# Gate and up products of sixteen experts: the eight high products of a block, then its eight low ones

## What is computed

```
gate, idx = lax.top_k(aff.T, cap)              # 16 experts, cap = 128 sample + 64 prompt tokens
xe  = h[idx]
hid = silu(einsum('ecd,edf->ecf', xe, w_gate)) * einsum('ecd,edf->ecf', xe, w_up)
ye  = einsum('ecf,efd->ecd', hid, w_down) * gate[..., None]
out = zeros_like(h).at[idx.reshape(-1)].add(ye.reshape(-1, D))
```

## Time and profile before

| | |
|---|---|
| median of three runs | 2502.47 us |
| the profiled execution | 2503.91 us |
| its span on the core | 2502.1 us |
| mean granted clock of PE | 0.986 |
| PE busy | 2428.1 us (97%) |
| PEld busy | 2170.2 us (87%) |
| DVE, ACT, POOL busy | 1678.2, 1459.8, 160.1 us |

### The profile page before, as it was taken

How to read it: one execution, slowest core, us unless ns; L and a number is a source line. 1 busy time by engine, 2 the same in 40 slices (tenths; PEclk the granted TensorE clock), 3 DMA queues, 4 the chain that set the end, 5 groups by cost and what they waited for, 6 DMA issues and landing times.

```text
span 2502.1 us, 42899 instructions
## 1 busy us (share of the span) xinstructions
PE 2428.1 (97%) x16262; PEld 2170.2 (87%) x16262; DVE 1678.2 (67%) x2520; ACT 1459.8 (58%) x2054; POOL 160.1 (6%) x168
## 2 busy tenths in 40 slices
PE   7999999989959999999999999999999999999997
PEld 6888867767659999898999989899998989999896
DVE  6355289854777667676666767676666767666676
ACT  4332188877645656655555656556565655656574
POOL 0000000000010101011010101101010110101010
PEclk9999999989979999999999999999999999999998
DMA  7353254354366767677676767767676776767695
GB/s 248 123 179 111 62 163 163 110 203 162 118 247 235 253 224 259 229 251 253 231 253 225 254 228 255 249 238 245 225 259 229 257 238 241 251 226 260 223 330 208
DMA packets 104548, 545.26 MB, mean 218 GB/s; under 512 B 11344, under 2 KB 19920, under 8 KB 54800
## 3 DMA queue, kind: packets, MB, share of 16 engines
q1 hardware_dynamic: 97072, 518.19, 58.9%
q0 software_dynamic: 7392, 25.96, 4.5%
HBM read 503.21 MB, written 40.89 MB: 217 GB/s over the span
## 4 chain that ended last, share of the span: by engine, by line
PE 69%; DVE 2%; ACT 1%; DMA 1%; issue 0%; POOL 0%; SPq 0%; DVEq 0%; ACTq 0%; POOLq 0%
PE ex_gate_ps L1938 16%; PE ex_up_ps L1938 16%; PE ex_gate_ps L1940 7%; PE ex_up_ps L1940 7%; PE ex_down_ps L1952 2%; PE ex_down_ps L1955 2%; PE ex_down_ps L1953 2%; PE ex_down_ps L1954 2%; PE ex_down_ps L1956 2%; PE ex_up_ps L1952 2%; PE ex_up_ps L1954 2%; PE ex_up_ps L1955 2%; PE ex_up_ps L1956 2%; PE ex_up_ps L1953 2%; PE ex_turn_ps L1914 0%; DMA fi_x<-acc_scratch 0%
## 5 line engine op out<-in xcount | busy, mean ns | idle before, releaser
L1793 DVE TENSOR_TENSOR ex_w_lo<-ex_w,ex_w_hi 128x2048 fp32r<-128x2048 f32 x384 | 879.9, 2292 | 450.3 <-ACT ex_w_hi L1705 444.2
L1705 ACT ACTIVATE ex_w_hi<-ex_w 128x2048 fp32r<-128x2048 f32 x384 | 733.5, 1910 | 209.4 <-PE ex_down_ps L1956 106.8
L1938 PE MATMUL ex_gate_ps<-ex_xt,ex_w_hi 128*128 128x384 f32 x2048 | 593.9, 360 | 1.8 <-DVE ex_xt L1799 1.8
L1938 PE MATMUL ex_up_ps<-ex_xt,ex_w_hi 128*128 128x384 f32 x2048 | 592.1, 359 | 0.0
L1940 PE MATMUL ex_gate_ps<-ex_xt,ex_w_lo 128*128 128x192 f32 x2048 | 513.6, 251 | 0.0
L1940 PE MATMUL ex_up_ps<-ex_xt,ex_w_lo 128*128 128x192 f32 x2048 | 512.7, 250 | 0.0
L1940 PEld LDWEIGHTS ex_gate_ps<-ex_xt,ex_w_lo 128*128 128x128 f32 x2048 | 392.3, 192 | 0.6
L1940 PEld LDWEIGHTS ex_up_ps<-ex_xt,ex_w_lo 128*128 128x128 f32 x2048 | 391.2, 191 | 0.0
L1938 PEld LDWEIGHTS ex_gate_ps<-ex_xt,ex_w_hi 128*128 128x128 f32 x2048 | 385.6, 188 | 2.5 <-issue 1.9
L1938 PEld LDWEIGHTS ex_up_ps<-ex_xt,ex_w_hi 128*128 128x128 f32 x2048 | 384.4, 188 | 0.0
L1725 ACT ACTIVATE ex_gate_low<-ex_gate_ps 128x384 f32<-128x384 f32 x128 | 63.0, 492 | 208.1 <-PE ex_gate_ps L1940 208.1
(11 more groups left out here) (298 smaller groups left out, 4011.4 us busy)
## 6 DMA issues: line engine op xcount, KB each, us to landing
ex_w<-in_w_experts SPq DMA_DIRECT2D x384, 1024.0 KB, 4.8
pj_w<-in_w_in SPq DMA_DIRECT2D x54, 512.0 KB, 3.7
pj_xr<-in_xt SPq DMA_DIRECT2D x12, 512.0 KB, 6.4
o_scratch<-ld_out SPq DMA_DIRECT2D x24, 256.0 KB, 4.1
at_bias<-in_near_bias SPq DMA_DIRECT2D x4, 1536.0 KB, 8.8
q_p<-in_x SPq DMA_DIRECT2D x12, 512.0 KB, 4.4
acc_scratch<-k_p SPq DMA_DIRECT2D x12, 512.0 KB, 5.3
h_scratch<-q_p SPq DMA_DIRECT2D x12, 512.0 KB, 2.9
```

The costliest lines, as they stand in the source:

```text
L1705: act.activation(w_hi[:, c % SLOTS, :], w[:, c % SLOTS, :], ACT.Copy).then_inc(hi_w, 1)
L1793: dve.tensor_tensor(w_lo[:, c % SLOTS, :], w[:, c % SLOTS, :], w_hi[:, c % SLOTS, :].bitcast(F32), ALU.subtract).then_inc(lo_w, 1)
L1938: nc.tensor.matmul(out[:, b, 0:2 * CAP], w_hi[:, slot, f], xt[:, k, :, :].rearrange("p h c -> p (h c)"), start=k == 0, stop=False)
```

## The change

Within a block the order of the sixteen matmuls changes. Before, the loop over the eight pieces issued a high and a low product for each piece. Now one loop issues the eight high products and a second one the eight low ones. The operands, the shapes and the number of instructions stay. The first product of a block still clears the bank, the last one is still a low product, and it raises the same semaphore.

```
                     for b in range(BLOCKS):
-                        for k in range(DT):
-                            f = slice((k * BLOCKS + b) * P, (k * BLOCKS + b + 1) * P)
+                        blocks = [slice((k * BLOCKS + b) * P, (k * BLOCKS + b + 1) * P) for k in range(DT)]
+                        for k, f in enumerate(blocks):
                             nc.tensor.matmul(out[:, b, 0:2 * CAP], w_hi[:, slot, f],
                                              xt[:, k, :, :].rearrange("p h c -> p (h c)"), start=k == 0, stop=False)
+                        for k, f in enumerate(blocks):
                             last = nc.tensor.matmul(out[:, b, 0:CAP], w_lo[:, slot, f], xt[:, k, 0, :],
                                                     start=False, stop=k == DT - 1)
                     last.then_inc(chunk_done, 1)
```

## The result

The changed kernel is slower: median 2510.92 us of seven runs (2509.84 to 2513.13), against 2503.04 us of seven runs before (2501.69 to 2505.68). The ratio is 1.0033, 95% interval 1.0022 to 1.0044, so 5.5 to 11 us, about a third of a per cent. The forecast was 2491 us, with 2484 to 2504 as its range.

The account below looks back on a forecast made before the run. PE alone was taken to bound the kernel. 3,584 low products saving 3.3 ns each gave 11.8 us, less 0.3 given back: 2503.9 - 11.5 = 2492.4, or 2491 us on the median's scale, range 2484 to 2504.

Parts of the forecast that it names:

- The cover of the sums and of the weights: Gate and up chunks: chunk sums and weight transfers stay early enough, so PE gets no idle time ahead of the lines.
- the split of the pair: Gate and up products: a pair's 284.4 ns divided into 170.6 for the high product and 113.8 for the low one.
- about 5 ns of latency that is paid once in a run: Low runs: part of each exposed load's 113.8 ns, beyond 109 ns of pace, would be paid by the first load alone.
- fifteen places: High products right behind a 512-column stream, their weights loaded in time; mean 170.6 ns to the next low product.
- The second source: An expert's last low product to line 1953: 340 ns less a 227 ns stream, giving 113 for the low product.
- (a): Transposes of 128 columns, showing loads in a row behind short streams: 110 ns a piece, near but not the same form.
- (b): The router's pair of 16-column matmuls: the second, a load behind a load, priced at 110 to 115 ns.
- the forecast's own case: Low runs: a later low product costs 108.5 to 112.4 ns, total 2484 to 2497.5 us, chance 0.61.
- x: Price of each of the seven low products behind another low one in a block, taken as 110.5 ns.
- Rival 2: Low runs slower: each slot waits for its load and one more hand-over, 118.5 ns, 17 us added, 2519; chance 0.10.
- Rival 1: Low runs: no change, the load behind a low product costs 113.8 ns wherever it stands, 2502.5 us; chance 0.26.
- Rival 3: Low runs much faster: loads overlap, price towards the 85 ns stream, 103 us off, 2399 us; chance 0.03.

Follow-up runs that it names:

- Low128_run: The changed kernel's runs of eight, but low products stream 128 columns instead of 192, leaving out part of the work; 2511.79 us in one run.
- gate_only: Against the kernel before, only gate chunks in runs of eight, up chunks still high and low in turn; 2508.82 us, ratio 1.0022.

## Why the prediction was wrong

**What bounds the kernel** was right: PE alone, no other engine, no transfer, before and after. The cover of the sums and of the weights held: no idle time ahead of the lines.

**The failed step is the split of the pair**, "384 columns take 170.6 ns" and so "a low product holds the engine for 113.8 ns", together with the "about 5 ns of latency that is paid once in a run" that came out of it. The 170.6 came from fifteen places, and all fifteen stand right behind a run of 512 columns. They are not the settled price: behind the same 512 columns the changed kernel's high run goes 171, 175, 178, 185, 176, 182, 173. Settled it is 173.3. The second source, 340 - 227 = 113, had the same flaw: it took the settled 227 for the first stream behind an exposed load, where experiments show first streams of a run to be a few ns longer.

In the prediction's terms a changed block is 8 x 170.6 + 113.8 + 7 x 110.5 = 2,252 ns. It takes 2,293. Of the 41 ns between them the high products make 36 to 39, depending on the reckoning (1,401 to 1,404 ns instead of 1,365), and the low ones 2 to 5 (889 to 892 instead of 887).

The prediction's own rows held another split: loads 109 ns apart behind a low product, which leaves 284.4 - 109 = 175.4 for the high one. The 4.8 ns between 113.8 and 109 were read as a latency of the load. There was none to save seven times a block: a low product in a long run costs 111.7, which is 0.6 ns more than in turn if the high product there is put at 173.3, and 3.4 ns more by the load starts (108.3).

**What came on top** was priced at nothing: "high products stay at 170.6". With high products at 173.3 in turn, the first three of a high run, 202 - 25, 176 and 182, cost some 15 ns more than three settled ones; the fit over the run lengths gives 13. By that fit a block loses 13 + 8 x 0.57 = 17.6 ns, times 512 blocks 9.0 us. Measured are 7.9 us between the medians. By the load starts the same 18 ns are a loss on the low products and a small gain on the high ones.

**Bounds and sources.** The transposes (a), 110 ns a piece, were a form of their own, and the router's pair (b) allowed 110 to 115 for the second of two. From each a price was taken off for a 512-column stream (231 ns, and 227 to 232), but the changed kernel's first such streams behind the exposed loads of a low run start 224 to 236 ns apart from the second on. With that range (a) is 109 to 112 a piece and (b)'s second product 106 to 118, so (b) decided nothing between 110.5 and 113.8. The low gaps of the changed kernel average 111.6. That is inside the forecast's own case (108.5 to 112.4), which stood for 2484 to 2497.5 us, and yet the kernel is slower: x alone didn't decide the time. What lay outside the bounds was the price of the other product.

**The rivals.** Rival 2 had the sign, slower, and the chance 0.10. The half of its mechanism that is a wait for the same columns of the bank falls by the alternating banks. The other half, a hand-over paid at each load behind a load, isn't excluded: it was priced at 4.7 ns, and the load starts show 3.3. Rival 1, an exposed load costs the same wherever it stands, is near for the low product if that costs 111.1 in turn (111.7 in a run), and not if it costs 108.3. Rival 3 needed 85 ns and got 111.7.

The Trainium skill, "TensorE: Matmul & The Clock Gate", section "Back-to-back issue gap", gives 81 ns as the sustained spacing of pairs of load and matmul at 128 columns. Low128_run contradicts it with a mean of 111.6. By the same section of the Trainium skill the gap of an isolated matmul of N columns at the full clock is N / 2.4 + 2.5, an estimate of 162.5 ns at 384 columns. The high runs, which are not isolated matmuls, settle at 173.3.

**The test I set myself** separated the cases: high products 171 apart if right, 175 and more if the first step was wrong. They were at 173 when settled and at 176 and 182 ahead of that. The loads of line 1941 start 111 to 112 ns apart behind the first one's 108, between "right" (110 to 111) and rival 1 (113 to 114). The time from first gate to first down product was to fall to about 72.1 us and rose to 73.37.

**Left open** is what in PE makes the steps, the slow start and the dearer low products behind low ones. The runs show that the order of the pieces and the banks have no part in it, and that the slow start shrinks when the load hardly sticks out. That the gaps of the changed kernel repeat this closely, whatever DVE, ACT and the transfers do beside them, speaks against these. That instructions might arrive late in low runs wasn't tried.

## What to carry to other kernels

Where each matmul has its own load of weights, reordering long and short products didn't hide more loads in these runs: every short one still exposed one. Here the order in turn was the cheapest of all that were tried with 192 columns. Take the price of a matmul from a long run of equal gaps, never from the first one behind another kind, and check it against the distance of the load starts: here the two differed by 5 ns, and the forecast took the difference for a saving. A step of 2 ns in a pair of matmuls decides 0.3% of this kernel, so a forecast built on such a difference needs that difference at the same column counts and in the same pattern.

## What the runs showed that was not expected

- Shortening a product can cost time. With 128 low columns instead of 192 the pair takes 286.7 ns instead of 284.4, as it does with 208: a step and not a slope.
- Nearly all chunk times are whole multiples of 13.33 ns (32 columns at 2.4 GHz): 4,573 is 343, 4,587 is 344, 4,613 is 346, 4,680 is 351, 4,693 is 352, 5,707 is 428 of them. The exceptions are 4,551, the order in turn with 160 or 192 columns, with 341.3, and the chunks of gate_only. In turn the gaps repeat over several pairs, and these stretches are whole multiples again: three pairs with 192 columns (285, 282 and 287 ns in rounded starts, 853.3 together, 64 of them), two with 128, 208 or 224 (573.3, 43), four with 256 (1,173.3, 88). So a mean pair comes in steps. Why the time comes in such units, no run explains.
- With 24 low products a run, whose program has 52,115 instructions instead of 42,899, PE waited at the start of 14 experts for some 2.5 us, which the profile puts down to issue, and the matmuls behind ran at the lower granted clock for some 4 us. That is why that kernel took 2858.2 us, where its chunks alone would make about 2,800. The wait, one such start in the timeline, and a window behind it:

```profile
PE ex_gate_ps L1942 <- issue: 34.1, 14, 2.6
```
```profile
848.31 0.39 PE L1961 MATMUL ex_up_ps<-ex_w_lo,ex_ht 128*128 128x512 f32 x1
851.22 0.64 PE L1942 MATMUL ex_gate_ps<-ex_xt,ex_w_hi 128*128 128x384 f32 x1 [2.52 <-issue]
851.65 1.64 PE L1945 MATMUL ex_gate_ps<-ex_xt,ex_w_lo 128*128 128x192 f32 x7
```
```profile
851.20:853.20 2.00, 1.99 (x9) 1.99 (x10) 0.00 (x0) 1.99 (x2) 1.70 (x2) 0.52 0.96 338
```

The window's granted clock is 0.52, near the level of 1.2 GHz.
